# Joined hi/lo products of 512 and 256 columns in the up projections of four MLPs

## The chip, the cores and the metric

The kernel runs on one core of a Trainium2 chip. The metric is the device time in microseconds of one execution; three executions of the kernel before gave 1311.13, 1312.89 and 1314.19 us, median 1312.89.

## The reference

Two transformer stacks of two layers each work on one sequence of T = 256 tokens with D = 1024 features, in fp32. The first stack has a differential attention layer and a sparse attention layer (NSA), each modulated by a condition vector c; the second has a latent attention layer (MLA) and a block attention layer (MoBA). Each of the four layers ends in the same kind of MLP with 4096 hidden features, called m0 to m3 here:

```
h = rms_norm(x, g)                      # m0, m1: then h * (1 + scale) + shift
x = x + gate * (square(relu(h @ w1)) @ w2)   # m2, m3: no gate
```

scale, shift and gate come from `silu(c) @ ada_w + ada_b`, a vector times a matrix of 1024 x 6144 per layer of the first stack (and one of 1024 x 2048 for the shared keys and values).

## The kernel before

**Precision.** A float32 product is made from three fp32r products (L538 to L540, `product`): with a = a_hi + a_lo and b = b_hi + b_lo it sums a_hi b_hi, a_hi b_lo and a_lo b_hi in PSUM. Weights are split when they arrive. A piece is 128 partitions x 1024 floats (512 KB). SyncE loads it into a ring of ten slots (`wring`), ScalarE copies its rounded high part into a ring of five (`whi`, L2765, `split_high`), VectorE subtracts to get the low part (`wlo`, L1619, `split_low`), and that subtraction frees the slot of `wring`. A piece can be split once TensorE has read the piece five places earlier.

**An MLP.** The hidden features are worked in eight chunks of 512. `up(c)` makes the hidden values of chunk c (feature-major: 128 features on the partitions, 256 tokens on the columns), from four pieces of w1, each with two of the eight k tiles and four blocks of 128 features. It is `by_pairs` (L558): two PSUM banks of 512 columns, each with two feature blocks of 256 columns, 96 products of 256 columns in all. `down(c)` multiplies chunk c with four pieces of w2 into four accumulating outputs in `ps_s` and `ps_p`, 48 products of 512 columns. The order on TensorE is up(0), up(1), down(0), up(2), down(1), ..., up(7), down(6), down(7). So a chunk is eight pieces: four of w1, then four of w2.

Between up(c) and down(c), for each half of a chunk (256 features, one bank): ScalarE takes ReLU of the bank into `hidden` (a tile in `ex`, three halves deep, L2891), then squares it into `g_hi` (L2896); GpSimd squares the same values in place in fp32 (L3460); VectorE subtracts to get `g_lo` (L1873).

**VectorE's order.** `mlp` on VectorE is a loop over 64 positions j, one per piece. At position j it does what is due (the two `g_low` come at the two positions behind the last w1 piece of a chunk), then in m0 and for two chunks in m1 one modulation sum (`matvec`, L1630: a piece of ada_w times the silu row, accumulated), then it splits the piece four places ahead. In m0 the sums fill positions 0 to 47: twelve modulation chunks of four pieces. In m2 `bias_steps` (L2438) adds the position-bias lookup: at j % 8 == 2 the one-hot comparisons (L2443, L2445), at j % 8 == 5 the addition of the mask that drains the lookup's bank (L2453). On TensorE `lookup` (48 products of 32 columns, L752) is called between up(c) and down(c-1) for c of 2 and more.

**Loads.** SyncE issues the loads in a fixed order, each when its ring slot is free. In m0 groups of four weight pieces and four modulation pieces alternate, so that a chunk has 16 loads; a modulation piece's slot is freed by its sum on VectorE. In the other MLPs a chunk has eight loads (m1 also has two modulation groups).

**Banks.** The four banks of `bank` are taken in turn (`bank_take`): TensorE waits until the last use of the bank is drained. In an MLP before, each up chunk takes two and ScalarE's ReLU drains them.

## Time and profile before

| | |
|---|---|
| median of three executions | 1312.89 us |
| profiled execution, its own time | 1313.38 us |
| its span, first to last instruction | 1311.6 us |
| TensorE busy | 1258.9 us, 96% |
| VectorE busy | 860.6 us, 66% |
| ScalarE busy | 691.9 us, 53% |
| GpSimd busy | 136.9 us, 10% |
| mean granted clock of TensorE | 0.991 |

Matmuls overlap, so the busy time of TensorE isn't a measure of its peak; the distance from one start to the next is. In the profile PE is the matmul, PEld the weight load, DVE is VectorE, ACT ScalarE, POOL GpSimd and SPq the queue of SyncE. The MLPs lie at 167 to 353, 532 to 718, 826 to 1018 and 1129 to 1308 us of the span. A row of the timeline gives the start, the duration, the engine, the line and what was written from what; in brackets stands the idle time of the engine before it and what ended it.

### The profile page before, as it was taken

Reading aid. Unit: us, or ns where it says so; the run is one execution under the profiler, and the core shown is the slowest. Engines: PE = TensorE matmul, PEld = TensorE weight load, DVE = VectorE, ACT = ScalarE, POOL = GpSimd, SP = SyncE. Lnnn points to the kernel's source line nnn. Section 1 sums busy time; section 2 is a strip of 40 time slices with the busy share of each in tenths; the row PEclk is TensorE's granted clock in tenths of the full one; section 3 lists DMA queues with packets and bytes.
Section 4 is the critical chain, followed back from the end, with each engine's and each line's share of the span. In section 5 each row is a group of like instructions: output and inputs, shape, how many; then the busy total and the mean of one; then the engine's idle time right before and its main releaser. Section 6 shows DMA issues by size and latency. Waiting matters only on the chain.

```text
span 1311.6 us, 21556 instructions
## 1 busy us (share of the span) xinstructions
PE 1258.9 (96%) x8320; PEld 1092.7 (83%) x8320; DVE 860.6 (66%) x1501; ACT 691.9 (53%) x1219; POOL 136.9 (10%) x154
## 2 busy tenths in 40 slices
PE   6899999999999999999999989999999999999999
PEld 4798799889799656889898867889998778899997
DVE  6578699898675675786546774665565566654444
ACT  3466454445455665644445874644444565654542
POOL 1012121121100000100100320100100100010100
PEclk7899999999999999999999999999999999999999
DMA  9879569999489151585653522686554554466650
GB/s 365 327 261 324 182 217 372 359 339 371 156 243 293 49 177 65 181 315 185 190 170 109 177 94 79 153 324 181 174 179 142 176 177 138 153 183 200 180 160 32
DMA packets 123780, 267.37 MB, mean 204 GB/s; under 512 B 11040, under 2 KB 33824, under 8 KB 123296
## 3 DMA queue, kind: packets, MB, share of 16 engines
q1 hardware_dynamic: 119328, 257.23, 59.1%
q0 software_dynamic: 1728, 6.29, 1.5%
q10 hardware_dynamic: 2624, 2.49, 0.6%
q8 instruction: 66, 1.08, 0.3%
q14 instruction: 34, 0.28, 0.1%
HBM read 264.83 MB, written 1.15 MB: 203 GB/s over the span
## 4 chain that ended last, share of the span: by engine, by line
PE 63%; DVE 5%; ACT 3%; issue 1%; POOL 1%; DVEq 0%; ACTq 0%; POOLq 0%
PE bank L538 12%; PE bank L540 11%; PE bank L539 11%; PE ps_s L538 3%; PE ps_s L539 3%; PE ps_s L540 3%; PE ps_p L538 3%; PE ps_p L539 3%; PE ps_p L540 3%; PE ps_s L1324 1%; DVE wlo L1619 1%; PE ps_p L1167 1%; PE ps_p L1143 1%; POOL rs L3444 1%; PE ps_s L1131 1%
## 5 line engine op out<-in xcount | busy, mean ns | idle before, releaser
L1619 DVE TENSOR_TENSOR wlo<-wring,whi 128x1024 fp32r<-128x1024 f32 (+1 forms) x376 | 457.9, 1228 | 262.5 <-ACT whi L2765 258.3
L2765 ACT ACTIVATE whi<-wring 128x1024 fp32r<-128x1024 f32 (+1 forms) x376 | 388.2, 1045 | 359.2 <-PE bank L540 135.1
L538 PE MATMUL bank<-h_hi,whi 128*128 128x256 f32 (+1 forms) x1224 | 348.7, 285 | 4.9 <-DVE wlo L1619 1.8
L539 PE MATMUL bank<-h_lo,whi 128*128 128x256 f32 (+1 forms) x1224 | 346.2, 283 | 0.0
L540 PE MATMUL bank<-h_hi,wlo 128*128 128x256 f32 (+1 forms) x1224 | 346.2, 283 | 0.0
L538 PEld LDWEIGHTS bank<-h_hi,whi 128*128 128x128 f32 (+1 forms) x1224 | 233.9, 191 | 10.7 <-issue 8.9
L539 PEld LDWEIGHTS bank<-h_lo,whi 128*128 128x128 f32 (+1 forms) x1224 | 234.0, 191 | 0.8
L540 PEld LDWEIGHTS bank<-h_hi,wlo 128*128 128x128 f32 (+1 forms) x1224 | 234.0, 191 | 0.0
L3460 POOL TENSOR_TENSOR ex<-ex 128x512 f32<-128x512 f32 x64 | 81.6, 1278 | 666.5 <-ACT g_hi L2896 666.5
L538 PE MATMUL bank<-whi,h_hi 128*128 128x512 f32 (+2 forms) x232 | 93.5, 403 | 12.8 <-DVE wlo L1619 10.4
L538 PE MATMUL ps_s<-whi,g_hi 128*128 128x512 f32 x256 | 101.0, 394 | 0.6 <-DVE wlo L1619 0.6
L538 PE MATMUL ps_p<-whi,g_hi 128*128 128x512 f32 x256 | 100.1, 391 | 0.0
L539 PE MATMUL ps_s<-wlo,g_hi 128*128 128x512 f32 x256 | 99.9, 390 | 0.0
L540 PE MATMUL ps_s<-whi,g_lo 128*128 128x512 f32 x256 | 99.7, 390 | 0.0
L540 PE MATMUL ps_p<-whi,g_lo 128*128 128x512 f32 x256 | 99.7, 389 | 0.0
L539 PE MATMUL ps_p<-wlo,g_hi 128*128 128x512 f32 x256 | 99.6, 389 | 0.0
L1630 DVE CUSTOM_DVE_ANT_0 wring<-wring,wide,params 128x1024 f32<-128x1024 f32 x64 | 85.2, 1337 | 7.1 <-DMA wring<-in_ada_w_t 7.1
L540 PE MATMUL bank<-whi,h_lo 128*128 128x512 f32 (+2 forms) x232 | 88.9, 383 | 0.0
L539 PE MATMUL bank<-wlo,h_hi 128*128 128x512 f32 (+2 forms) x232 | 88.9, 383 | 0.0
L1873 DVE TENSOR_TENSOR g_lo<-ex,g_hi 128x512 fp32r<-128x512 f32 x64 | 46.3, 724 | 34.5 <-POOL ex L3460 34.5
L538 PEld LDWEIGHTS bank<-whi,h_hi 128*128 128x128 f32 x232 | 44.8, 193 | 24.1 <-issue 14.6
L538 PEld LDWEIGHTS ps_s<-whi,g_hi 128*128 128x128 f32 x256 | 48.1, 188 | 10.7 <-DVE wlo L1619 0.9
(391 smaller groups left out, 1763.5 us busy)
## 6 DMA issues: line engine op xcount, KB each, us to landing
wring<-in_mlp_w SPq DMA_DIRECT2D x128, 512.0 KB, 5.2
wring<-in_mlp_w_in SPq DMA_DIRECT2D x64, 512.0 KB, 3.9
wring<-in_mlp_w_out SPq DMA_DIRECT2D x64, 512.0 KB, 4.0
wring<-in_ada_w_t SPq DMA_DIRECT2D x48, 512.0 KB, 8.0
wring<-in_ada_w SPq DMA_DIRECT2D x36, 512.0 KB, 6.3
wring<-in_moba_w_qkv SPq DMA_DIRECT2D x24, 512.0 KB, 3.9
wring<-in_a_qk SPq DMA_DIRECT2D x16, 512.0 KB, 7.2
wring<-in_kv_ada_w_t SPq DMA_DIRECT2D x16, 512.0 KB, 6.9
```

The lines of the kernel that those rows point to most:

```text
L538: nc.tensor.matmul(out, lh, rh, start=first, stop=False, skip_group_check=mixed)
L539: nc.tensor.matmul(out, lh, rl, start=False, stop=False, skip_group_check=mixed)
L540: return nc.tensor.matmul(out, ll, rh, start=False, stop=last, skip_group_check=mixed)
L1131: last = nc.tensor.matmul(ps_s[:, m, lo:lo + n], q_t[rows, j, t * P:(t + 1) * P], k_nsa[rows, w, j // 2, 0:n], start=True, stop=True)
L1143: last = nc.tensor.transpose(ps_p[:, 0, i * P:(i + 1) * P], ex[:, 2 * (b % 2) + m, i * P:(i + 1) * P], ident[:, :])
L1167: last = nc.tensor.matmul(out_[m][:, lo:lo + n], v_nsa[:, w, i, g * 64:(g + 1) * 64], pt_nsa[b % 2][:, m, at:at + n], start=False, stop=(w ...
L1324: last = nc.tensor.matmul(ps_s[:, u % 2, lo:lo + n], q[:, t * P:(t + 1) * P], k[:, 0:n], start=(i == 0), stop=(i == len(parts) - 1))
L1619: v.tensor_tensor(piece_view(wlo, p), raw_view(p), piece_view(whi, p).bitcast(F32), ALU.subtract).then_inc(lo_ready, 1)
L1630: return v.tensor_tensor_reduce(w, w, c_row[:, :], 1.0, params[:, at:at + 1], ALU.mult, ALU.add, mod[:, 4 * i + j:4 * i + j + 1])
L1873: v.tensor_tensor(g_lo[at], hidden[:, b % 3, :].rearrange("p (i t) -> p i t", t=T), g_hi[at].bitcast(F32), ALU.subtract).then_inc(sem("mlp ...
L2765: a.activation(piece_view(whi, p), raw_view(p), ACT.Copy).then_inc(hi_ready, 1)
L3460: g_.tensor_tensor(h, h, h, ALU.mult).then_inc(sem("mlp_sq"), 1)
```

## The change

`h_hi` and `h_lo` become two halves of one tile, `h_both`. In all four MLPs `up(c)` is made by `by_halves`: each block of 128 features has a whole bank. The high weights are multiplied with high and low activations in one product of 512 columns (columns 0 to 255 get w_hi h_hi, columns 256 to 511 get w_hi h_lo), and the low weights with the high activations in one of 256 columns, added to the second half. A chunk has 64 products instead of 96, and takes all four banks.

The two halves of a bank must be added. ScalarE copies the second half into `rest` (in the tile `att`), VectorE adds the first half to it (`join`, at the position behind the last w1 piece), which drains the bank; ScalarE then takes ReLU in place and squares. `g_low` comes one position later. In m2 the lookup moves from ahead of down(c-1) into its middle, and the addition behind it from j % 8 == 5 to 3.

```diff
-        h_hi = sb("h_hi", [P, KT, T], F32R)
-        h_lo = sb("h_lo", [P, KT, T], F32R)
+        h_both = sb("h_both", [P, 2, KT, T], F32R)
+        h_hi, h_lo = h_both[:, 0, :, :], h_both[:, 1, :, :]
...
+        JOINED = ["m0", "m1", "m2", "m3"]
+        rest = att[:, 0:D].rearrange("p (i t) -> p i t", t=T)
...
+            def by_halves(key, ready=None):
+                banks = [bank_take(pe, key + (n,)) for n in range(4)]
+                for j in range(KT // 2):
+                    p = piece_wait()
+                    wh, wl = piece_view(whi, p), piece_view(wlo, p)
+                    for n in range(4):
+                        out = bank[:, banks[n], :]
+                        for k in (2 * j, 2 * j + 1):
+                            if ready and n == 0:
+                                ready(k)
+                            at = (slice(None), k % 2, slice(n * P, (n + 1) * P))
+                            nc.tensor.matmul(out, wh[at], h_both[:, :, k, :], start=(k == 0), stop=False,
+                                             skip_group_check=True)
+                            last = nc.tensor.matmul(out[:, T:2 * T], wl[at], h_hi[:, k, :], start=False,
+                                                    stop=(k == KT - 1), skip_group_check=True)
+                        if n < 3 and j == KT // 2 - 1:
+                            last.then_inc(filled[banks[n]], 1)
+                    piece_over(last, key + (3,) if j == KT // 2 - 1 else None)
...
-                def down(c):
+                def down(c, middle=None):
                     pe.wait_ge(sem("mlp_glo"), 16 * int(tag[1]) + 2 * c + 2)
                     if c < 7:
                         for k in range(4):
+                            if middle and k == 2:
+                                middle()
...
-                    if beside and c >= 2:
-                        beside(c - 2)
-                    down(c - 1)
+                    down(c - 1, (lambda: beside(c - 2)) if beside and c >= 2 else None)
...
+                def join(c):
+                    for n in range(4):
+                        i, key = 4 * c + n, (f"{tag}_w1", c, n)
+                        if n % 2 == 0 and 2 * c + n // 2 >= 3:
+                            dve.wait_ge(sem("mlp_glo"), 16 * int(tag[1]) + 2 * c + n // 2 - 2)
+                        dve.wait_ge(sem("mlp_rest"), 32 * JOINED.index(tag) + i + 1)
+                        src = bank_full(dve, key)
+                        v.tensor_tensor(hidden[:, (2 * c + n // 2) % 3, (n % 2) * T:(n % 2 + 1) * T], src[:, 0:T],
+                                        rest[:, i % 4, :], ALU.add).then_inc(drained[uses[key][0]], 1)
...
                 for j in range(64):
                     p = base + j
+                    if j in joins:
+                        join(joins[j])
                     if j in due:
                         g_low(due[j])
                     key = pieces[p][0]
                     if key[0].endswith("w1") and p == first_piece[key] + 3:
-                        due.update({j + 1: 2 * key[1], j + 2: 2 * key[1] + 1})
+                        behind = 2 if tag in JOINED else 1
+                        due.update({j + behind: 2 * key[1], j + behind + 1: 2 * key[1] + 1})
+                        if tag in JOINED:
+                            joins[j + 1] = key[1]
...
-                if j % 8 == 5 and 0 <= j // 8 - 2 < LOOKUPS:
+                if j % 8 == 3 and 0 <= j // 8 - 2 < LOOKUPS:
...
+            def joined_mlp(tag):
...
+                for c in range(8):
+                    for n in range(4):
+                        i, key = 4 * c + n, (f"{tag}_w1", c, n)
+                        src = bank_full(act, key)
+                        if c:
+                            bank_emptied(act, (f"{tag}_w1", c - 1, n))
+                        a.activation(rest[:, i % 4, :], src[:, T:2 * T], ACT.Copy).then_inc(sem("mlp_rest"), 1)
+                    for half in range(2):
+                        b = 2 * c + half
+                        for n in (2 * half, 2 * half + 1):
+                            bank_emptied(act, (f"{tag}_w1", c, n))
+                        h = hidden[:, b % 3, :]
+                        a.activation(h, h, ACT.Relu).then_inc(sem("mlp_relu"), 1)
+                        if c >= 2:
+                            act.wait_ge(*read_end[first_piece[(f"{tag}_w2", c - 2)] + 3])
+                        act.wait_ge(sem("mlp_relu"), 16 * JOINED.index(tag) + b + 1)
+                        a.activation(g_hi[:, c % 2, 2 * half:2 * half + 2, :], h.rearrange("p (i t) -> p i t", t=T),
+                                     ACT.Square).then_inc(sem("mlp_ghi"), 1)
```

## Rows read from the trace of the kernel before

**Rows 1.** The page: busy time and share by engine; the chain that ended last.
```profile
PE 1258.9 (96%) x8320; PEld 1092.7 (83%) x8320; DVE 860.6 (66%) x1501; ACT 691.9 (53%) x1219; POOL 136.9 (10%) x154
...
PE 63%; DVE 5%; ACT 3%; issue 1%; POOL 1%; DVEq 0%; ACTq 0%; POOLq 0%
```

**Rows 2.** Timeline of TensorE in m1: start and duration in us, line, what.
```profile
565.76 0.28 PE L538 MATMUL bank<-h_hi,whi 128*128 128x256 f32 x1
...
577.27 0.40 PE L538 MATMUL ps_s<-whi,g_hi 128*128 128x512 f32 x1
...
588.18 0.28 PE L538 MATMUL bank<-h_hi,whi 128*128 128x256 f32 x1
```

**Rows 3.** Windows of m0: length, busy time by engine, granted clock, DMA share, GB/s.
```profile
190.37:305.86 115.49, 113.08 (x722) 102.42 (x721) 107.05 (x128) 50.77 (x58) 17.83 (x10) 1.00 0.97 356
```

**Rows 4.** Waits from 165 to 370 us: in total, times, longest.
```profile
ACT whi L2765 <- DMA wring<-in_mlp_w: 71.2, 43, 6.2
...
DVE wlo L1619 <- ACT whi L2765: 19.0, 14, 3.1
```

**Rows 5.** 128x256 instructions from PSUM, VectorE and ScalarE: min/median/max ns.
```profile
L2498 DVE TENSOR_TENSOR h_lo<-ps_p,h_hi x8: 416/423/425, 778.6 to 815.1; 128x256 fp32r<-128x256 f32 x8
...
L3272 ACT ACTIVATE bias<-bank x8: 366/379/399, 746.9 to 771.9; 128x256 f32<-128x256 f32 x8
```

**Rows 6.** Timeline of VectorE in m0.
```profile
187.29 0.68 DVE L1873 TENSOR_TENSOR g_lo<-ex,g_hi 128x512 fp32r<-128x512 f32 x1
...
194.57 2.05 DVE L1619 TENSOR_TENSOR wlo<-wring,whi 128x1024 fp32r<-128x1024 f32 x1
...
264.39 2.06 DVE L1619 TENSOR_TENSOR wlo<-wring,whi 128x1024 fp32r<-128x1024 f32 x1
266.37 1.52 DVE L1873 TENSOR_TENSOR g_lo<-ex,g_hi 128x512 fp32r<-128x512 f32 x1
267.82 1.27 DVE L1630 CUSTOM_DVE_ANT_0 wring<-wring,wide,params 128x1024 f32<-128x1024 f32 x1
...
269.02 1.22 DVE L1619 TENSOR_TENSOR wlo<-wring,whi 128x1024 fp32r<-128x1024 f32 x1
270.16 0.68 DVE L1873 TENSOR_TENSOR g_lo<-ex,g_hi 128x512 fp32r<-128x512 f32 x1
...
280.65 1.23 DVE L1619 TENSOR_TENSOR wlo<-wring,whi 128x1024 fp32r<-128x1024 f32 x1 [1.58 <-ACT whi L2765]
...
312.10 2.05 DVE L1619 TENSOR_TENSOR wlo<-wring,whi 128x1024 fp32r<-128x1024 f32 x1
```

**Rows 7.** Timeline of ScalarE in m0, behind up(4).
```profile
262.07 0.58 ACT L2891 ACTIVATE ex<-bank 128x512 f32<-128x512 f32 x1
262.68 0.63 ACT L2896 ACTIVATE g_hi<-ex 128x512 fp32r<-128x512 f32 x1
263.22 0.58 ACT L2891 ACTIVATE ex<-bank 128x512 f32<-128x512 f32 x1
...
267.41 1.06 ACT L2765 ACTIVATE whi<-wring 128x1024 fp32r<-128x1024 f32 x1 [2.95 <-DMA wring<-in_mlp_w]
```

**Rows 8.** Timeline of GpSimd and VectorE in m1, behind up(0).
```profile
544.87 1.23 POOL L3460 TENSOR_TENSOR ex<-ex 128x512 f32<-128x512 f32 x1 [0.40 <-ACT g_hi L2896]
545.84 1.34 DVE L1619 TENSOR_TENSOR wlo<-wring,whi 128x1024 fp32r<-128x1024 f32 x1 [0.65 <-ACT whi L2765]
```

**Rows 9.** The page, loads of m2 and m3: count, KB each, us from issue to landing.
```profile
wring<-in_mlp_w_in SPq DMA_DIRECT2D x64, 512.0 KB, 3.9
```

**Rows 10.** Timeline of TensorE in m0, the first product of up(5).
```profile
270.38 0.36 PE L538 MATMUL bank<-h_hi,whi 128*128 128x256 f32 x1 [0.84 <-DVE wlo L1619]
```

**Rows 11.** Timeline of VectorE in m2, chunk 2: one-hot pair, next split, bias addition.
```profile
881.20 0.81 DVE L2443 TENSOR_SCALAR extra<-arena,cmp_w 128x2048 f16<-128x2048 f16 x1
...
883.30 1.23 DVE L1619 TENSOR_TENSOR wlo<-wring,whi 128x1024 fp32r<-128x1024 f32 x1
...
889.51 0.68 DVE L2453 TENSOR_TENSOR bias<-bank,wide 128x512 f32<-128x512 f32 x1
```

More of the change, by code:

```diff
@@ L576, in by_pairs @@
                     piece_of[key + (g,)] = p
+            def by_halves(key, ready=None):
[17 more added lines that the diff above has]
+                for n in range(4):
+                    piece_of[key + (n,)] = p
             def by_token(key, src, kt, readers=1, first_k=0, between=None, apart=False, step=None):
@@ L761, in up @@
                 def up(c):
+                    if tag in JOINED:
+                        by_halves((f"{tag}_w1", c), (lambda k: wait(tag, k)) if c == 0 else None)
+                        return
                     by_pairs((f"{tag}_w1", c), (h_hi, h_lo), (lambda k: wait(tag, k)) if c == 0 else None)
@@ L1865, in mlp @@
                 base = first_piece[(f"{tag}_w1", 0)]
-                due = {}
+                due, joins = {}, {}
+                def join(c):
[7 more added lines that the diff above has]
+                                        rest[:, i % 4, :], ALU.add).then_inc(drained[uses[key][0]], 1)
                 def g_low(b):
@@ L2882, in attention @@
                             copy(u - 1)
+            def joined_mlp(tag):
+                if tag in x_sums:
+                    act.wait_ge(sem("x_squared"), 2 * list(x_sums).index(tag) + 2)
+                for c in range(8):
+                    for n in range(4):
+                        i, key = 4 * c + n, (f"{tag}_w1", c, n)
[14 more added lines that the diff above has]
+                                     ACT.Square).then_inc(sem("mlp_ghi"), 1)
+                keep_ahead("act", first_piece[(f"{tag}_w2", 7)])
             def mlp(tag):
+                if tag in JOINED:
+                    joined_mlp(tag)
+                    return
                 for b in range(2 * FF // W):
```

1 line of the change is left out of this document (added).

## The prediction

> **What bounds the kernel now.** I read the busy times first, then the chain, then TensorE's order of time inside one MLP, and last the waits and timelines of VectorE and ScalarE in the first MLP. TensorE is busy for 96% of the span, and 63% of the chain that ended last is its own [rows 1]. In the second MLP it runs without a gap: 96 products of an up chunk from 565.76 to 577.27, 48 of a down chunk from there to 588.18 [rows 2]. The third and fourth MLPs repeat this. The first MLP differs: five chunks take 115.49 us, where 11.51 + 10.91 each [rows 2] would make 112.1, with the DMA engines 97% busy [rows 3], ScalarE waits 71.2 us there for weights, and VectorE 19.0 us for ScalarE's high parts [rows 4]. TensorE, the DMA stream and VectorE are all close to their limit in it. So the change has to be priced per MLP.
>
> **TensorE: three products become two.** Before, 96 products of 256 columns take 11.51 us, 119.9 ns each; 48 of 512 columns take 10.91 us, 227.3 ns each [rows 2]. At the full granted clock of 2.4 GHz [rows 3] the columns alone would be 106.7 and 213.3 ns. Each product thus costs some 13.2 to 14.0 ns on top of its columns, whatever its width. The new pair (512, then 256) streams the same 768 columns in 227.3 + 119.9 = 347.2 ns against 359.7: 12.5 ns less, in 8 chunks x 32 pairs x 4 MLPs = 1024 pairs, 12.8 us in all, 3.2 us an MLP, 0.4 us a chunk. Nothing in the trace shows a 512-column operand read as two runs of 256 far apart. Bounds: all 12.8 us, or nothing if that reading costs the 12.5 ns again. I take the full gain, because the two widths agree on the fixed part.
>
> **ScalarE and VectorE: the added work.** Per chunk ScalarE gets four 128x256 copies (379 ns each), VectorE four 128x256 additions from PSUM (416 to 425 ns) [rows 5]. VectorE's consecutive instructions start some 0.08 us before the end of the previous one (a 680 ns g_lo costs 0.60 [rows 6]), so four joins occupy 1.36 us. ScalarE has room everywhere (53% busy [rows 1]). The second new thing is order. ReLU now waits for a join, and the high part of the piece behind the chunk is queued on ScalarE behind two ReLUs and two squares. By the steps of before (0.61 and 0.54 us from start to start [rows 7]; an SBUF source makes the first about 0.63) ScalarE starts that high part 2.4 us after it is released by the second join, it takes 1.06 us [rows 7], and 0.1 us later VectorE can subtract. I cost this at nothing in the second and fourth MLP: TensorE has four split pieces in hand when the join begins (one down chunk, 10.9 us [rows 2]), VectorE is through after about 5 us. g_lo of the last chunk comes about 8 us after the last up product and is needed after 10.9. The copies run while the last piece of the chunk is still multiplied. These two MLPs gain 3.2 us each.
>
> **The first MLP.** Here each of 48 positions of VectorE's loop also holds a modulation sum. One position, subtraction and sum, is 2.34 us (267.82 to 270.16: 1.20 and 1.14) [rows 6]. A chunk of eight is 18.7, with two g_lo of 0.60 each 19.9. GpSimd's squares slow two VectorE instructions a chunk: 2.06 instead of 1.22, 1.52 instead of 0.68, 1.7 us in all. The rest, 1.58 and more at the first piece of a w2 group, is a wait for weights [rows 6]. From 194.57 to 312.10 five chunks take 117.5, 23.5 each [rows 6].
> After: 19.9 + 1.36 of joins. Then VectorE runs joins 3 and 4 and one sum (1.9 us) against ScalarE's chain of 3.7 us, and idles 1.8. But GpSimd's squares now fall mostly into that idle time. In the second MLP, where a subtraction starts at 545.84 while GpSimd works from 544.87 to 546.10, it takes 1.34 instead of 1.22 [rows 8]; I take 0.2 us a chunk instead of 1.7. That makes 23.3. The wait for weights: a load issued when its ring slot is freed lands after 3.9 us if little is queued [rows 9], its high part adds 1.3, and VectorE has 4.7 us of other work before it needs it: 0.5 us at least. The queue adds to it. A chunk is 16 loads of 0.524 MB, at 356 GB/s and 97% share [rows 3] 22.9 us of full use; VectorE's longer first half lets the queue drain, and I get 0.1 to 0.3 more. So 24.0 us a chunk against 23.5, though 3 us were added. Bounds of the chunk: 23.5, if the transfers alone pace it; 26.4, if the 1.7 of GpSimd stays and the wait for weights is 1.6 as before.
> At the start, g_lo of the second half moves behind one more position and the join: it comes at 191.9 instead of 187.97 [rows 6], TensorE starts its first down product at 192.0 instead of 190.37, and VectorE is 0.8 us late four positions on. TensorE then follows VectorE: it has lost its margin, as it waited 0.84 us for a subtraction before already [rows 10]. From there 4.6 chunks x 0.5 = 2.3 more, and the last up chunk, behind the sums, gives 0.4 back: 0.8 + 2.3 - 0.4 = **+2.7 us**. By the bounds: +0.4 and +13.7.
>
> **The third MLP.** The bucket lookup (48 products, 1.2 us) moves from behind the up chunk to the middle of the down chunk, since all four banks are taken until the joins are through, and VectorE's bias addition from the sixth to the fourth position of a chunk. The next up chunk now asks for all four banks at once, the lookup's among them. With TensorE's end of the up chunk as zero, VectorE goes: joins to 1.0, subtraction from 4.1 (ScalarE's chain), g_lo, subtraction, g_lo, subtraction to 8.8, the one-hot pair 2.10 (881.20 to 883.30 [rows 11]) to 10.9, subtraction to 12.1, bias addition 0.68 [rows 11] to 12.8. TensorE wants the banks at 10.91 + 1.2 + 0.1 = 12.2. That is 0.7 us of stall in five chunks (the sixth lookup is followed by no up chunk), 3.5 us, bounds 0 and 1.2 each. The MLP changes by -3.2 + 3.5 = **+0.3 us** (-3.2 to +2.8).
>
> **Sum.** +2.7 - 3.2 + 0.3 - 3.2 = -3.4 us on the profiled execution's 1313.38 (span 1311.6 and 1.8 around it). The median of before is 0.5 lower; the same step from it gives **1309.5 us**.
>
> **A rule of the Trainium skill on the first step.** The rows give some 13 ns of fixed cost per product [rows 2]. The Trainium skill, TensorE: Matmul & The Clock Gate, section "Wait — 56ns, not 53.3ns?", puts the fixed part of a warm product at about 2.5 ns. By that page the joined pair would save 2.5 ns, 2.6 us over the kernel instead of 12.8, 0.65 an MLP, and the kernel would come out near 1317.5. The measured rows decide for my sum; the trace doesn't show whether the 13 ns belong to the product or to the weight load ahead of it, but both go from three to two.
>
> **The rivals.**
> *VectorE becomes the bound of the first MLP by more (slower).* GpSimd's squares keep slowing VectorE by 1.5 us a chunk more than I take: a cycle of 25.5. Then 0.8 + 4.6 x 2.0 - 0.4 = +9.6 there, in sum +3.5: 1316.5 us. For it: VectorE is already busy 107.1 of 115.5 us [rows 3]. Against: its new idle time lies where GpSimd works. It decides above 24.7 us a chunk.
> *The joined product gains nothing (slower).* The two far runs cost the 12.5 ns again, or the fixed cost isn't one of the product. Then +3.1 + 0 + 3.5 + 0 = +6.6: 1319.5 us. For it: no row shows such an operand. Against: the fixed part is the same at both widths.
> *The transfers pace the first MLP and the lookup's bank is in time (faster).* +0.4 - 3.2 - 3.2 - 3.2 = -9.2: 1303.7 us. For it: the DMA engines are 97% busy [rows 3], so VectorE's waits could swallow all the joins; the bias addition misses by 0.7 us only. Against: the waits seen (19.0 us [rows 4]) lie in the other half of the chunk than the new ones.
>
> **How the numbers follow.** Forecast 0.5, with a range of its own from 1306 to 1314; VectorE bound 0.25; no gain on TensorE 0.08; all hidden 0.17. Range with 8 in 10: 1304 to 1318. A measurement of this kernel tells about 0.2%, 2.6 us, from no change. Of the forecast's half, 0.29 lies below that and 0.19 inside; the hidden case is faster; the two slower ones leave 0.04 inside. Faster 0.46, within 0.23, slower 0.31.
>
> **What would show it.** Up chunks of the second and fourth MLP 11.1 us instead of 11.5, with no gap. The first down product of the first MLP near 192, and VectorE's cycle there near 24.0, with idle time behind the joins. In the third MLP a wait of TensorE for VectorE's bias addition, of some 0.7 us, five times. It would be wrong if the up chunks stay at 11.5, if the second or fourth MLP shows waits for split weights or g_lo, or if the cycle of the first is 25 or more.

## The result, and the profile after

The changed kernel takes 1329.8 us (median of 1328.6, 1331.6, 1331.0 and 1325.9), the kernel before 1313.5 beside it: a ratio of 1.0111, 95% interval 1.0093 to 1.0129. I had forecast 1309.5 with a range of 1304 to 1318. It is slower by 16 us, outside the range and on the wrong side.

The page after: busy time by engine, and the chain of work that ended last.
```profile
PE 1256.6 (95%) x7296; PEld 1038.3 (78%) x7296; DVE 883.9 (67%) x1629; ACT 731.7 (55%) x1347; POOL 122.6 (9%) x154
...
PE 58%; DVE 8%; ACT 3%; issue 2%; POOL 1%; DVEq 0%; ACTq 0%; POOLq 0%
```
Compared with [rows 1], TensorE issues 1024 products fewer and yet is busy almost as long; VectorE's share of the chain rises from 5 to 8%. Where the time went is read best from the first product of each MLP in the two timelines:

| | before starts | after starts | this MLP and what lies behind it | forecast |
|---|---|---|---|---|
| m0 | 167.26 | 167.36 | +10.8 | +2.7 |
| m1 | 531.74 | 542.64 | 0.0 | -3.2 |
| m2 | 826.35 | 837.26 | +4.5 | +0.3 |
| m3 | 1128.77 | 1144.17 | -0.2 | -3.2 |

Three readings lie under it. First, TensorE in m0 behind up(0), and VectorE in the same stretch (start, duration, what; in brackets the idle time before it and what ended it):
```profile
178.50 0.28 PE L594 MATMUL bank<-h_both,wlo 128*128 128x256 f32 x1
...
182.83 1.41 DVE L1903 TENSOR_TENSOR ex<-bank,att 128x256 f32<-128x256 f32 x4
...
184.50 0.76 PE L592 MATMUL bank<-h_both,whi 128*128 128x512 f32 x1 [5.72 <-DVE ex L1903]
...
185.27 0.63 PE L592 MATMUL bank<-h_both,whi 128*128 128x512 f32 x1
185.70 0.41 PE L594 MATMUL bank<-h_both,wlo 128*128 128x256 f32 x1
185.91 0.63 PE L592 MATMUL bank<-h_both,whi 128*128 128x512 f32 x1
```
up(1) follows up(0) directly, and its first product waits for all four banks, hence for all four joins of chunk 0. VectorE reaches them only at 182.83, behind its sums and splits. The same wait is there in the other MLPs, 1.2 to 1.3 us each. I had no such term at all: the first two up chunks take 31.04, 24.20, 24.00 and 24.00 us, against 23.11 before. The wait costs more than its 5.7 us: behind it the pairs come 0.64 us apart (185.27 to 185.91) and not 0.35. The granted clock says why. The window from 167.30 to 190 (length, busy PE, PEld, DVE, ACT, POOL, granted clock, DMA share, GB/s) has it at 0.85:
```profile
167.30:190.00 22.70, 16.92 (x81) 14.54 (x82) 20.81 (x33) 11.66 (x17) 2.29 (x2) 0.85 0.67 229
```

Second, TensorE in m1, one up chunk (as [rows 2]):
```profile
599.98 0.39 PE L592 MATMUL bank<-h_both,whi 128*128 128x512 f32 x1
...
611.27 0.40 PE L540 MATMUL ps_s<-whi,g_hi 128*128 128x512 f32 x1
```
11.29 us for 32 pairs, 352.8 ns each, where I had 347.2. The pair saves 6.9 ns and not 12.5.

Third, ScalarE and VectorE in m0 around a chunk's end:
```profile
268.31 1.19 ACT L2937 ACTIVATE att<-bank 128x256 f32<-128x256 f32 x4
...
271.81 1.41 DVE L1903 TENSOR_TENSOR ex<-bank,att 128x256 f32<-128x256 f32 x4
...
272.65 0.63 ACT L2943 ACTIVATE ex<-ex 128x512 f32<-128x512 f32 x1 [3.16 <-DVE ex L1903]
...
275.16 2.94 ACT L2808 ACTIVATE whi<-wring 128x1024 fp32r<-128x1024 f32 x3
...
276.31 1.23 DVE L1646 TENSOR_TENSOR wlo<-wring,whi 128x1024 fp32r<-128x1024 f32 x1 [1.89 <-ACT whi L2808]
```
ScalarE stands 3.16 us for VectorE's joins, and after the two Relus and Squares VectorE stands 1.89 us for ScalarE's high half. The waits of 165 to 370 us say how much that is in all:
```profile
ACT whi L2808 <- DMA wring<-in_mlp_w: 46.7, 25, 7.2
DVE wlo L1646 <- ACT whi L2808: 31.9, 22, 4.2
...
ACT ex L2943 <- DVE ex L1903: 18.7, 6, 4.5
```
ScalarE waits less for loads than in [rows 4] (46.7 for 71.2), VectorE more for ScalarE (31.9 for 19.0), and the wait of 18.7 is new.

### The profile page after: what moved, and what is told of

Same layout as the page of the kernel before. It is cut to its first block, busy times and chain, and to the rows that moved or that the text cites. A ratio compares the mean times of both kernels' runs of the same rounds, so it can differ in the third digit from the quotient of the medians.

```text
span 1326.8 us, 20048 instructions
## 1 busy us (share of the span) xinstructions
PE 1256.6 (95%) x7296; PEld 1038.3 (78%) x7296; DVE 883.9 (67%) x1629; ACT 731.7 (55%) x1347; POOL 122.6 (9%) x154
## 4 chain that ended last, share of the span: by engine, by line
PE 58%; DVE 8%; ACT 3%; issue 2%; POOL 1%; DVEq 0%; ACTq 0%; POOLq 0%
PE bank L592 14%; PE bank L594 7%; PE bank L540 5%; PE bank L542 4%; PE bank L541 4%; PE ps_s L540 3%; PE ps_s L542 3%; PE ps_s L541 3%; PE ps_p L542 3%; PE ps_p L540 3%; PE ps_p L541 3%; DVE wlo L1646 2%; PE ps_s L1351 1%; ACT whi L2808 1%; PE ps_p L1194 1%
## 5 line engine op out<-in xcount | busy, mean ns | idle before, releaser
L592 PE MATMUL bank<-h_both,whi 128*128 128x512 f32 x1024 | 365.9, 401 | 21.7 <-DVE ex L1903 9.6
L594 PE MATMUL bank<-h_both,wlo 128*128 128x256 f32 x1024 | 288.3, 282 | 0.0
L592 PEld LDWEIGHTS bank<-h_both,whi 128*128 128x128 f32 x1024 | 193.5, 189 | 73.9 <-issue 26.8
L594 PEld LDWEIGHTS bank<-h_both,wlo 128*128 128x128 f32 x1024 | 194.6, 190 | 0.6
L3530 POOL TENSOR_TENSOR ex<-ex 128x512 f32<-128x512 f32 x64 | 67.9, 1063 | 700.8 <-ACT g_hi L2947 700.0
L540 PE MATMUL bank<-whi,h_both 128*128 128x512 f32 (+2 forms) x232 | 93.6, 403 | 13.2 <-DVE wlo L1646 10.7
L541 PE MATMUL bank<-wlo,h_both 128*128 128x512 f32 (+2 forms) x232 | 89.0, 384 | 0.0
L542 PE MATMUL bank<-whi,h_both 128*128 128x512 f32 (+2 forms) x232 | 89.0, 384 | 0.0
L540 PEld LDWEIGHTS bank<-whi,h_both 128*128 128x128 f32 x232 | 44.9, 193 | 24.3 <-issue 14.8
L540 PE MATMUL bank<-h_both,whi 128*128 128x256 f32 (+1 forms) x200 | 58.6, 293 | 0.0
L2937 ACT ACTIVATE att<-bank 128x256 f32<-128x256 f32 x128 | 46.9, 380 | 17.7 <-PE bank L594 17.2
L541 PE MATMUL bank<-h_both,whi 128*128 128x256 f32 (+1 forms) x200 | 56.5, 282 | 0.0
```

The lines of the kernel that those rows point to most:

```text
L540: nc.tensor.matmul(out, lh, rh, start=first, stop=False, skip_group_check=mixed)
L541: nc.tensor.matmul(out, lh, rl, start=False, stop=False, skip_group_check=mixed)
L542: return nc.tensor.matmul(out, ll, rh, start=False, stop=last, skip_group_check=mixed)
L592: nc.tensor.matmul(out, wh[at], h_both[:, :, k, :], start=(k == 0), stop=False, skip_group_check=True)
L594: last = nc.tensor.matmul(out[:, T:2 * T], wl[at], h_hi[:, k, :], start=False, stop=(k == KT - 1), skip_group_check=True)
L2937: a.activation(rest[:, i % 4, :], src[:, T:2 * T], ACT.Copy).then_inc(sem("mlp_rest"), 1)
```

## The experiments

The table gives for each kernel the ratio to the kernel before (95% interval), and from its profile m0: its first two up chunks, the rest to the end of the last up product, and their sum, in us. All the stretches are read from the starts of TensorE's products. The ratio rests on all executions of a kernel, the stretches on the profiled one alone.

| kernel | ratio | first two | rest | sum |
|---|---|---|---|---|
| before | 1 | 23.1 | 138.2 | 161.3 |
| changed | 1.0111 (1.0093-1.0129) | 31.0 | 140.2 | 171.3 |
| e1 banks one by one | 1.0068 (1.0049-1.0088) | 28.7 | 146.3 | 175.0 |
| e2 chunk 0 plain | 1.0034 (1.0017-1.0052) | 23.6 | 144.5 | 168.1 |
| e3 m0 old | 1.0034 (1.0023-1.0046) | 23.1 | 138.0 | 161.1 |
| e4 sums later | 1.0127 (1.0110-1.0144) | 24.0 | 140.3 | 164.3 |
| e5 splits first | 1.0044 (1.0028-1.0059) | 30.0 | 138.1 | 168.2 |
| e6 m0 old, banks one by one | 0.9981 (0.9971-0.9991) | 23.6 | 136.9 | 160.5 |
| e7 contiguous | 0.9983 (0.9968-0.9998) | 23.1 | 136.8 | 159.9 |
| e9 plain and splits | 1.0024 (1.0011-1.0038) | 22.9 | 146.7 | 169.6 |
| e10 one split | 1.0042 (1.0027-1.0057) | 22.9 | 149.1 | 172.0 |
| e11 wide first | 0.9939 (0.9922-0.9956) | 23.1 | 138.1 | 161.2 |
| e13 joined, short sums | 0.9949 (0.9932-0.9967) | 23.5 | 133.4 | 156.8 |
| e14 old, short sums | 0.9954 (0.9938-0.9969) | 23.6 | 134.5 | 158.1 |
| e15 joined, short loads | 1.0008 (0.9996-1.0021) | 30.0 | 135.7 | 165.8 |
| e16 old, short loads | 0.9951 (0.9935-0.9967) | 23.1 | 134.5 | 157.6 |

Two rows can therefore differ by some microseconds without their kernels doing so. e1's six executions lie between 1318.9 and 1326.6 us, with mean granted clocks of 0.991 and 0.986 at the two ends, and the profiled one is the slowest; e2's twelve lie between 1313.4 and 1323.7, and the profiled one took 1315.2. A part of this is TensorE's clock. In e1 two up chunks of m0, in e2 and e4 one, have a mean granted clock of 0.87 and take 12.74 to 12.77 us, where the others at 1.00 take 11.29 to 11.65. In e2 the wait ahead of the slow one is
```profile
224.82 0.50 PE L594 MATMUL bank<-h_both,whi 128*128 128x512 f32 x1 [1.87 <-DVE wlo L1648]
```
The same is seen between m1 and m2. That stage runs wholly at the full clock in the profiles of before, of the changed kernel, of e2 and of e3; in the other twelve a part near 760 to 800 us is at the lower level, and the stage is 1.6 or 3.2 us longer. Whether a change brings that about isn't shown.

**e1, banks one by one.**
```diff
-                banks = [bank_take(pe, key + (n,)) for n in range(4)]
+                banks = []
...
+                        if j == 0:
+                            banks.append(bank_take(pe, key + (n,)))
```


> The changed kernel, but each of the four banks of an up chunk is taken (and waited for) just before its own first product, not all four before the first product of the chunk. Theory: the up chunk that directly follows another up chunk (chunk 1 behind chunk 0, once an MLP) waits for the fourth and last join of chunk 0, 1.2 to 1.3 us in m1, m2 and m3 and 5.7 us in m0. A join needs 0.35 us, and the second bank is wanted only 0.7 us (two pairs) after the first: so the wait falls by the three later joins, 1.05 us in m0 (4.7 us stay, since VectorE only gets to the first join that late) and by all of 1.2 us in each of the other three. Total -4.7 us, 1325.1 us, a ratio to before of 1.0075 instead of 1.0111. Rival: VectorE and ScalarE pace the chunks and the wait at the start only moves lateness that comes back at the first down product; then less than 1 us comes back in all, 1329 us, ratio 1.0107.


Measured: 1323.8 us. TensorE's waits from 540 to 1010 us (m1, m2 and what lies between) held two rows for banks in the changed kernel:
```profile
PE bank L592 <- DVE bias L2496: 4.0, 5, 0.9
PE bank L592 <- DVE ex L1903: 2.5, 2, 1.3
```
In e1 the first row is gone and the second is down to 0.2 us. m1 (to its last up product) and m3 gave 1.2 and 1.3 us, as expected, though the stage behind m1 took 3.1 us more in this profile, by the clock; m2 gave 5.9, because the lookup's bank is now wanted last of four and its bias addition is in time. m0 did the opposite: 2.4 us gained on the first two chunks, 6.1 lost behind them. Of the 6.1, the two up chunks at 0.87 are 3.0, and TensorE's waits for low halves, 8.2 us for 5.6, are most of the rest. The bank wait is shown as the cause for m1 to m3, and for m0 not beyond its start. The 1325.1 us of the forecast came out near, but by other parts: more in m2, less in m0.

**e2, chunk 0 in the old way** (two banks, three products, Relu from the bank), on top of e1.
```diff
-                    if tag in JOINED:
+                    if tag in JOINED and c:
                         by_halves((f"{tag}_w1", c))
...
-                for c in range(8):
+                for b in range(2):
...
+                    a.activation(hidden[:, b, :], src, ACT.Relu).then_inc(drained[uses[key][0]], 1)
...
+                    a.activation(g_hi[:, 0, 2 * b:2 * b + 2, :], hidden[:, b, :].rearrange("p (i t) -> p i t", t=T),
+                                 ACT.Square).then_inc(sem("mlp_ghi"), 1)
+                for c in range(1, 8):
```


> The kernel of the experiment before, and chunk 0 of each MLP is made in the old way (three products of 256 columns a pair, two banks, Relu straight from the bank by ScalarE, no rest copies and no joins); chunks 1 to 7 stay joined. Theory: the changed kernel's first two up chunks cost 31.0 us in m0 and 24.0 in the others, against 11.5 + 11.3 = 22.8 without a wait for banks. m1, m2 and m3 give 1.2 us each. In m0 TensorE's stall of 5.7 us goes, but VectorE is next: between its joins of chunk 0 (182.83) and chunk 1 (198.13) it needed 15.3 us for four positions, where a chunk of eight takes 24.7; without the stall four positions are 12.3 us, and the four joins of chunk 0 (1.4 us) go, so join 1 comes 4.4 us earlier and all of m0 with it. Total -8.0 us: 1321.8 us, ratio 1.0050. Rival 1, VectorE's own load is all of m0's loss: only the 1.4 us of its joins go there, 1324.8 us. Rival 2, the bank wait was the whole loss of m0: the first down product comes at 191.0 instead of 198.4 and stays 7.4 us ahead, 1318.8 us.


Measured: 1318.3 us. The start of m0 is repaired (23.6), but 144.5 us follow where the changed kernel had 140.2. Of 7.5 us gained, 3.2 stay. One up chunk at the lower clock is 1.5 of the 4.3 lost, 2.0 are longer waits for low halves (7.5 us for 5.6). So the forecast of 4.4 us for m0 was too high; 1321.8 us was beaten because it left out the 4 us behind m2's lookups.

**e3, m0 as before.** `JOINED = ["m1", "m2", "m3"]`


> The changed kernel with m0 left as it was before (m1, m2 and m3 joined). Theory: m0 starts at the same time in both traces and ends 10.9 us later in the changed one, so all of that comes back and nothing else moves: 1318.9 us, ratio 1.0028, and what stays (+3.5 to +5 us) is m2. Rival: the lateness of m0 is partly made up by transfers that run ahead meanwhile, which the later stages then lack when it is gone; then 3 to 5 us of the 10.9 stay, 1322 to 1324 us.


Measured: 1317.7 us, ratio 1.0034 for the 1.0028 expected; m1 starts at 531.47. All of m0's loss comes back, and nothing is lost elsewhere for it.

**e4, sums later.**
```diff
-    plan += mix(mlp("m0"), ada(0, range(10, 12)) + ...)
+    m0 = mlp("m0")
+    plan += m0[:2] + mix(m0[2:], ada(0, range(10, 12)) + ...)
...
-            mlp("m0", ada_order[10:22], last=...)
+            mlp("m0", ada_order[10:22], last=..., first=8)
```


> The changed kernel, but the twelve sums of m0 begin behind chunk 1 (VectorE's positions 8 to 55 instead of 0 to 47, their loads behind the second up chunk), as m1's two do. Theory: TensorE's 5.7 us wait in m0 is there because VectorE does four sums (1.28 us each) and four splits (1.23 us) ahead of the first join; without the sums it is at that join when the bank is full, and the wait is the 1.2 us of m1. The eight first positions then take 24.0 us in place of 31.0; but eight sums move into a chunk that had none (22.3 us then, 24.7 with sums), so 2.4 us come back later: -4.6 us, 1325.2 us, ratio 1.0076. Rival: TensorE waits for the joins as such, not for the sums ahead of them: the wait stays near 5.7 us, and only the order of the sums changes, 1330 to 1332 us.


Measured: 1331.0 us. The reading of the trace was right and the forecast wrong: the wait fell to 1.2 us (24.0 for the first two chunks), so it was the sums ahead of the join. But 8 us came back behind the last up chunk, where sums now lie: m1 starts at 543.49, in the changed kernel at 542.64. Part of that is clock again: the window from 345 to 375 us has it at 0.83, the changed kernel from 353 to 383 at 0.94. The rival's 1330 to 1332 us was met, but not for its reason, since the wait did fall. Here the repaired start was worth nothing by itself.

**e5, one high half ahead of each Relu**, on top of e1.
```diff
                     for half in range(2):
                         b = 2 * c + half
+                        keep_ahead("act", first_piece[(f"{tag}_w1", c)] + 4 + half)
```


> The kernel with banks taken one by one (m0 joined, first sums at position 0), and ScalarE copies one high half of a later piece ahead of the first Relu of a chunk and one ahead of the second, instead of all of them behind both pairs of Relu and Square. Theory of a handshake: in m0 of the changed kernel ScalarE is through with the rest copies of a chunk at 269.5, stands 3.16 us in front of Relu until VectorE's four joins (271.81), then does 2.7 us of Relu and Square, and only then the next high half (275.16), for which VectorE in turn stands 1.89 us (276.31): once a chunk, each waits for the other. Over m0 VectorE's idle time in front of its low halves grew from 19.0 to 31.9 us, while its busy time did not grow: that 12.9 us is the 10.9 us of m0. With a high half ready ahead of Relu the wait of 1.9 us goes in seven chunks: 8 to 11 us of m0 come back, 1314 to 1316 us, ratio about 1.001. Rival 1, transfers: in the same stretch the DMA engines are busy 0.93 of the time, and the slots in which loads land come free as VectorE works; then the wait only turns into one for a load, and less than 3 us come back, 1321 to 1324 us. Rival 2, VectorE's added joins (32 x 0.35 = 11.3 us) are the loss: nothing comes back.


Measured: 1320.2 us. VectorE's waits of 165 to 365 us:
```profile
DVE g_lo L1913 <- POOL ex L3533: 11.1, 11, 1.1
DVE wlo L1648 <- ACT whi L2810: 10.8, 14, 2.6
```
Its wait for high halves fell from 34.8 us in e1 to 10.8, and the stretch behind the first two chunks from 146.3 to 138.1. From m0's start to m1's it is 371.2 us for 378.6. But the ratio, over all executions, fell by 0.0024 only, 3.2 us: e1's profile is of its slowest execution. The forecast of 8 to 11 us missed, and 3.2 is close to the first rival's less than 3. A new wait of 11.1 us for GpSimd's square came in.

**e9 and e10, both repairs, and one split only.** e9 is e2 with e5's line; e10 has `+ 4` for `+ 4 + half`.


> Both repairs of m0 together: chunk 0 in the old way (no wait of up chunk 1 for joins) and one high half ahead of each of the two Relus of a chunk; banks one by one, all four MLPs joined. Theory (two separate losses that add up): the profile with the splits moved had 138.1 us for m0's chunks behind the first two, as before's 138.2, but 30.0 us for the first two, where the one with a plain chunk 0 had 23.6 and before 23.1. Together 23.6 + 138.1: m0 takes what it took before, and m1, m2, m3 are 1.2, 1.1 and 1.3 us shorter than before. Sum -3 us against before: 1310 to 1311 us, ratio 0.9977; against the kernel with m0 left old it is a tie. Rival: m0's chunks are held up by VectorE's total work whatever the order, and once the start is early the lateness comes back behind it, as with banks one by one (2.4 us gained at the start, 6.1 us lost behind it); then 138 becomes 142 to 145 us, and the ratio is 1.002 to 1.004.

> As the one before, but only one high half of a later piece ahead of the first Relu of a chunk, none ahead of the second. In the profile with both, VectorE stood 11.1 us (11 times, up to 1.1) in front of the difference of a half block for GpSimd's square, which it never did in the changed kernel: the second copy makes the second Square 1.06 us late. Theory: with one copy only, that wait goes, and VectorE's wait for high halves (10.8 us with both, 31.9 with none) grows less than that, since the next piece is already there: m0 is 1 to 3 us shorter than in the experiment beside it, ratio 0.996. Rival: the waits change places one for one, the two kernels agree within 1 us.


Measured: 1318.9 and 1322.1 us. The repairs don't add: with the start at 22.9 us, the rest took 146.7 and 149.1, the rival's case in e9. In e10 the wait for GpSimd fell from 9.2 to 7.3 us and that for high halves rose from 15.7 to 19.6; both forecasts for e10 missed. By then seven kernels with joined m0 had ended it at 164 to 175 us, the one of 164 giving it back later, and what sets that total was still open.

**e13 to e16, less work for VectorE or fewer bytes, in joined and in old m0.** In e13 and e14 m0's modulation sums take 128 of 1024 columns; in e15 and e16 their loads bring 128 of them, and the sums stay whole. Part of the modulation is left out in all four.
```diff
-                ins = mod_block(key, j, loaded(load)[:, 0, :])
+                ins = mod_block(key, j, loaded(load)[:, 0, 0:P] if key in ada_order[10:22] else ...)
...
+                if key in ada_order[10:22]:
+                    to, src = to[:, :, 0:P], src[:, :, 0:P]
                 sp.dma_start(to, src)
```


> All four MLPs joined, banks one by one; VectorE's sums of m0 take only 128 of their 1024 columns (part of the modulation is left out), their loads stay whole. So VectorE has about 1.1 us less to do in each of 48 positions. Theory VectorE: what holds joined m0 is that VectorE comes late to the joins and splits; then the start wait goes (22.9 us for the first two chunks) and the rest is set by the loads as before's m0 was: 160 to 162 us from m0's start to its last up product where the kernel with whole sums has 171 to 175; -11 to -14 us of 1323.8, 1310 to 1313 us, ratio 0.998. Theory transfers: the slots come free later only because loads come later; m0 stays at 168 us or more, ratio 1.004 or more.

> m0 old, m1 to m3 joined, banks one by one, and the same short sums. Theory: before's m0 is set by its loads (DMA engines busy 0.97 of the time) and not by VectorE: from its start to the last up product 160 to 161 us as with whole sums (161.3), ratio 0.998 as with whole sums. Rival: VectorE's work (166 us busy of the 171 to 198) is what sets it already before; then it falls to the 157.6 us of m1's pace, -4 us, ratio 0.995.

> All joined, banks one by one, and the sums' loads bring only 128 of their 1024 columns (the sums run over all columns of what lies in the slot; part of the modulation is left out), so m0's transfers fall from 58.7 to some 36 MB. Theory VectorE: VectorE does as much as before and waits no less in front of the first joins, but the loads come in time: the waits for high halves that come from late loads go, and VectorE's busy time of 164 us with the start wait remains; 165 to 170 us to the last up product, ratio 1.003. Theory transfers: m0 falls to TensorE's pace, 22.9 + 133.4 = 156 to 158 us, ratio 0.995.

> m0 old with the same short loads, m1 to m3 joined. Theory: the loads set before's m0, so it falls to TensorE's pace of 23.1 + 134.5 = 157.6 us from 161.3, if VectorE (153 us of busy time in these 48 positions and behind them) lets it: ratio 0.995. Rival: VectorE set it; it stays at 161 us, ratio 0.998.


Windows of 190 to 310 us (length, busy PE, PEld, DVE, ACT, POOL, granted clock, DMA share, GB/s), for the changed kernel,
```profile
190.00:310.00 120.00, 116.08 (x583) 97.10 (x583) 103.74 (x148) 58.12 (x79) 11.34 (x10) 1.00 0.91 328
```
e13, joined with short sums,
```profile
190.00:310.00 120.00, 120.00 (x601) 101.34 (x600) 76.67 (x158) 67.32 (x89) 12.48 (x12) 1.00 1.00 380
```
and e15, joined with short loads:
```profile
190.00:310.00 120.00, 119.90 (x606) 101.02 (x605) 108.33 (x152) 60.12 (x81) 11.36 (x10) 1.00 0.60 199
```
With short sums and every byte still loaded, joined m0 takes 156.8 us, TensorE has no gap, and the DMA engines bring 380 GB/s. So the transfers could do more than either kernel asked of them, and the DMA share of 0.91 is not their limit. Joined and old m0 are then about even (156.8 and 158.1 us, where old m0 loses 0.5 at its start at a clock of 0.98; 1307.3 and 1308.0 us for the whole kernels).

With short loads and whole sums the start still costs 30.0 us, 4.0 of it the wait for the joins. VectorE's sums ahead of the first joins are its cause, as e4 says too. Behind the start it is different: 135.7 us, where e1 had 146.3, the changed kernel 140.2, and e13 133.4. There fewer bytes help nearly as much as fewer sums, though VectorE does all its work. So neither VectorE's work nor the bytes alone hold up these chunks, but both together. That fits the ring, though no run separates its parts: a slot comes free when VectorE is through with it, and through ScalarE VectorE waits for what lands in it. From e1, whose edit both kernels have, the ratio falls by 0.0119 with short sums and by 0.0060 with short loads.

Joined m0 with short loads (165.8) stays 8.1 us behind old m0 (157.6). Old m0 misses TensorE's pace of 157.6 us by 2.3 to 3.7 with whole sums and whole loads, and by 0.5 or none when either is cut. My forecast for e14, that only the loads set it, was wrong, and so was the same idea in e13, where I had 160 to 162 us for joined m0.

**e6, m0 old with e1's edit; e7, the two halves of h side by side; e8 and e12, products alone; e11, another order.** e6 joins `["m1", "m2", "m3"]`; e7 has `h_both = sb("h_both", [P, KT, 2, T], F32R)` on top of e6.


> m0 in the old way, m1, m2 and m3 joined with their banks taken one by one. From the profiles of the two experiments this is put together of: m0 as before; m1 and m3 1.2 and 1.5 us shorter than before (22.9 and 133.4 us against 23.1 and 134.5), m2 1.1 us shorter, since taking the banks one by one also took away the 0.8 us that TensorE stood behind each of five lookups (the lookup's bank is the last of the four that the next up chunk takes). Theory: these add up, -3.8 us, 1310 us, ratio 0.9971. Rival: what the first up chunks give comes back later, as m0's did, and the kernel is as before, ratio 1.000.

> The kernel of the experiment before with the high and the low half of a k tile of h side by side in memory (one run of 512 columns) instead of 8 KB apart (two runs of 256). Theory: the 5.6 ns that a joined pair costs above the 347.2 ns of my sum are the jump between the two runs; then up chunks fall from 11.29 to 11.11 us (64 pairs instead of 64 times 352.8 ns: 22.2 to 22.58), 24 chunks, -8.6 us at 352.8 - 347.2 = 5.6 ns for 32 x 2 pairs a chunk, that is 0.36 us each where TensorE paces them; 1301 to 1306 us. Rival: a product's cost above its columns does not depend on where its columns lie; pairs stay at 352.8 ns and the time equals that of the experiment before within 1 us.

> Only products, nothing of the reference is computed: TensorE alone, stretches of 64 pairs each (three products of 256 columns; 512 + 256 with the 512 in two runs; 512 + 256 with them side by side; 512 and 256 into two banks; 512 alone in two runs, 512 alone side by side, 256 alone, 384 alone; then the first two kinds again). Theory from the two traces: three products cost 359.7 ns and the joined pair 352.8 ns here too, without any other engine at work; if each product costs its columns and the same 13.2 ns, 512 alone is 226.5, 384 alone 173.2 and 256 alone 119.9 ns and the joined pair would be 346.4; so either 512 alone comes out at 232.9, or the pair costs more than its two parts. Rival 1: the 6 ns are the jump between two runs, 512 side by side is 226.5 and in two runs 232.9. Rival 2: they are the second product's partial write into the bank just written: into two banks the pair is 346.4. Rival 3: they come from the other engines' traffic, and the pair alone is 346.4.


e6 took 1311.5 us, 0.9981 for the 0.9971 expected. In its profile m1 (to its last up product), m2 and m3 are 1.2, 1.0 and 1.3 us shorter than before, so the parts add up; the stage behind m1 is 3.2 us longer, by the clock. e7 took 1311.8, no difference, and its up chunks stay at 11.29. (Its forecast counted 64 pairs a chunk; there are 32, so the theory was worth 4.3 us and not 8.6. It fails either way.) e8's timeline at the borders of its stretches (64 pairs or products each, all at a granted clock of 1.00; `far` is the operand in two runs, `near` in one):
```profile
63.40 0.40 PE L78 MATMUL bank<-far,w_hi 128*128 128x512 f32 x1
...
86.01 0.40 PE L83 MATMUL bank<-near,w_hi 128*128 128x512 f32 x1
...
108.63 0.40 PE L88 MATMUL bank<-far,w_hi 128*128 128x512 f32 x1
...
131.24 0.40 PE L93 MATMUL bank<-far,w_hi 128*128 128x512 f32 x1
...
145.77 0.39 PE L97 MATMUL bank<-near,w_hi 128*128 128x512 f32 x1
...
160.28 0.28 PE L101 MATMUL bank<-far,w_hi 128*128 128x256 f32 x1
...
167.95 0.34 PE L105 MATMUL bank<-near,w_hi 128*128 128x384 f32 x1
...
179.05 0.28 PE L72 MATMUL bank<-far,w_hi 128*128 128x256 f32 x1
...
202.08 0.40 PE L78 MATMUL bank<-far,w_hi 128*128 128x512 f32 x1
```
Divided by 64: the pair 353.3 ns in two runs, 353.4 in one, 353.3 into two banks; 512 alone 227.0 in two runs and 226.7 in one, 256 alone 119.8, 384 alone 173.4, three of 256 together 359.8. The parts are what I took. The pair in turn costs 6.5 ns more than its parts, with no other engine at work; all three rivals fall.


> Only products again, nothing of the reference; 128 in a stretch, each into its own columns of a bank with its own weights: 512 and 256 in turn, by twos, by fours, by eights, then 512 and 384, 512 and 128, 256 and 128 in turn, 128 alone, and three of 512 to one of 256. Theory: a change of length costs 3.3 ns a change, whichever way: 512 and 256 in turn 353.3 ns for two, by twos 350.0, by fours 348.4, by eights 347.6; three to one 227.0 x 3 + 119.8 + 6.5 = 807.3 ns for four. Rival 1: it is the load of weights that must fit beside the product ahead of it: then 256 behind 512 is cheap and 512 behind 256 dear, and the sums are the same, but 512 and 384 in turn cost no extra (400.4 ns for two). Rival 2: products in turn always cost 3.3 ns each, in any grouping: by eights 353 ns.


e12, in ns for one of each: 512 and 256 in turn 353.4, by twos 348.4, by fours 350.9, by eights 349.1 (parts 346.8); 512 and 384 in turn 413.1 (parts 400.4); 512 and 128 in turn 339.4, 256 and 128 in turn 231.4, 128 alone 111.6 (parts 338.6 and 231.4); three of 512 to one of 256, 812.8 for four (parts 800.8). Grouping is cheaper than turn about, but there is no price per change of length: twos beat fours, and 512 with 384 costs 12.7 ns extra where 512 with 256 costs 6.5. That refutes the theory (348.4 ns by fours, 347.6 by eights) and both rivals (no extra with 384; 353 ns by eights). What it is stays open.
In e11 the 512s of a piece go ahead of its 256s (the code is shortened):
```diff
+                    turns = [(0, 1), (2, 3)] if j == KT // 2 - 1 else [(0, 1, 2, 3)]
+                    for ns in turns:
+                        for n in ns:
+                            for k in ks:
+                                nc.tensor.matmul(bank[:, banks[n], :], wh[at], h_both[:, :, k, :], ...)
+                        for n in ns:
+                            for k in ks:
+                                last = nc.tensor.matmul(bank[:, banks[n], T:2 * T], wl[at], h_hi[:, k, :], ...)
```


> m0 old, m1 to m3 joined with banks one by one, and the products of a piece in another order: the eight of 512 columns first, then the eight of 256 (in the last piece of a chunk four and four, so that the first banks are full early). Theory from products alone: 512 columns again and again cost 227.0 ns, 256 again and again 119.8, but the pair in turn 353.3 ns, 6.5 ns more than its parts; so it is the change of length from one product to the next that costs, and eight and eight pay it once, not eight times: 5.5 ns less a pair, 32 pairs in 8 chunks of three MLPs, 4.2 us less than the same kernel with pairs in turn: up chunks of 11.11 us for 11.29, 1307.3 us, ratio 0.9950. Rival: the extra is there for any product of 256 columns that adds into a bank's second half between others, in any order; then the chunks stay at 11.29 us and the ratio at 0.998.


In e11's m1 an up chunk is
```profile
564.62 0.39 PE L596 MATMUL bank<-h_both,whi 128*128 128x512 f32 x1
...
575.78 0.40 PE L540 MATMUL ps_s<-whi,g_hi 128*128 128x512 f32 x1
```
11.16 us, 4.1 ns less a pair. I had expected 5.5; e12's groups of eight say 4.3. 1308.1 us, ratio 0.9939 (0.9922 to 0.9956): the lowest ratio of all, and the fastest of the kernels that leave nothing out. Its profile is 3.1 us shorter than e6's; the ratios say 5.5, but their intervals together allow 3.1.

## Why the prediction was wrong

From the start of m0 to the end the profile is 15.1 us longer where I had 3.4 shorter. Of that difference 8.1 us lie in m0, 3.2 in m1, 4.2 in m2 and 3.0 in m3.

**The step that failed: "I cost this at nothing".** In the part on the added work of ScalarE and VectorE I followed the join into the down chunk, where TensorE has four split pieces in hand, and never into the chunk pair up(0), up(1), where no down chunk lies between. There TensorE wants the banks at once. It cost 1.2 to 1.3 us in each of m1 to m3, which e1 took away, and in m0 5.7 us of waiting and some 2.6 more at the lower clock behind it. I had seen the banks asked for all at once in m2 and priced it only there.

**The first MLP, +2.7 for +10.8.** Of the 10.8 us, 7.9 lie in the first two up chunks (31.04 for 23.11) and 2.9 behind them. I took the first down product at 192.0, 1.6 us later than before, and it came at 198.40. The 7.9 are the wait for the joins and what came of it. e13, with a wait of 0.7 there, takes 23.5, so 22.8 without any. 31.0 less 22.8 and less 5.7 leaves some 2.6 us. That fits the stretch up to 190 us in which the pairs came 0.64 us apart for 0.35.

The walk of VectorE itself was near in its parts: the second g_lo at 192.36 for 191.9, joins of 1.41 us, an idle time of 1.8 to 1.9 us in front of the next high half behind six of the eight joins, GpSimd's squares no longer in the way (the two g_lo of a chunk take 0.68 to 0.69 us; [rows 6] has one of 1.52). From join to join its cycle was 24.2 to 25.3 us, 24.6 on average, for the 24.0 I had. That is just short of the 24.7 from which I let the rival of a bound VectorE begin. The rival's +9.6 for m0 lies close to the +10.8 by luck: nearly all of it is a cycle 2.0 us longer in each chunk. The cycle was 1.1 us longer (24.6 for 23.5), and of TensorE's 10.8 us only 2.9 lie behind the start.

What sets joined m0 is shown for the start: VectorE's sums ahead of the first joins (e4 and e13 take the wait to 1.2 and 0.7 us, e15 leaves 4.0). Behind the start it is VectorE's sums and the loads together, each of which gives most of it back when cut (e13, e15). Another order alone did not mend it: e1, e2, e4, e5, e9 and e10 all stay above the kernel before. Why the chunks behind an early start take longer (144.5 to 149.1 in e2, e9 and e10, for 138.1 and 140.2 in e5 and the changed kernel) is settled in part. TensorE stands 7.5, 8.3 and 11.0 us there for low halves, against 2.4 and 5.6, and one, two and one of its up chunks run partly at the lower clock (one in e5 too). Why VectorE is late with the low halves isn't settled; from 190 to 310 us the DMA share is 0.89 to 0.92 in all five.

**The pair: right mechanism, wrong size.** 12.5 ns expected, 6.9 measured, 1.8 us an MLP for 3.2. I added the costs of two products measured each among its own kind; in turn they cost 6.5 ns more. The rival of no gain is wrong as well, and the reason it gave, two far runs, is refuted by e7 and e8. The Trainium skill's rule from the prediction (TensorE: Matmul & The Clock Gate, section "Wait — 56ns, not 53.3ns?": some 2.5 ns of fixed cost) isn't what these products show, each with its own weight load: 13.1 ns above the columns at 256, 13.7 at 512. Of the pair's saving it would have left 2.5 ns, and 6.9 were measured.

**The third MLP, +0.3 for +4.5.** The stall behind the lookup was there, five times, 0.8 us for 0.7 (my own terms, 12.8 less 12.2, give 0.6). VectorE and TensorE at that place:
```profile
920.13 0.68 DVE L2496 TENSOR_TENSOR bias<-bank,wide 128x512 f32<-128x512 f32 x1
...
921.07 0.47 PE L592 MATMUL bank<-h_both,whi 128*128 128x512 f32 x1 [0.67 <-DVE bias L2496]
```
The rest is the pair's size (1.4 us), the wait behind up(0) (1.2) and the lookups themselves: in the middle of a down chunk each takes 1.35 us (e1, m2 against m1), and 1.22 before.

**Second and fourth MLP, -3.2 for 0.0 and -0.2.** The pairs cost 1.4 us more than I had, the one bank wait 1.2 to 1.3, and the down chunks take 10.94 to 10.95 us for 10.91.

## What to carry to other kernels

Where a change takes more buffers at once, look for the place where two producers follow each other with nothing between, and take each buffer just before its own first use; here that was worth 1.2 to 1.3 us in three of the MLPs and 4 us behind the lookups. A stage in which an engine is busy 93% of the time, and hands work to another in a fixed order, is no place for work moved off TensorE: price it by how often each waits for the other, and by what a wait of TensorE costs in clock, and leave it out if in doubt. When two resources are both close to their limit, cut each by itself before naming one as the cause. Before two profiles are compared, see where each lies among the executions of its kernel. Measure an operation in the sequence in which it will run, not among its own kind.

## What the hardware showed that I had not expected

Products of 512 columns cost 227 ns among themselves and products of 256 cost 120, but in turn 353.3 for the two, and 512 with 384 in turn 12.7 ns more than their parts. With weights of its own a product of 128 columns costs 111.6 ns, hardly less than one of 256. Reading the operand as two runs 8 KB apart costs at most 0.3 ns. After the wait of 5.7 us in m0 the granted clock is 0.85 in the window 167.3 to 190 and 1.00 in the next one, against 1.00 in both before: below 1.00 means that a part of that stretch ran at the lower of the two levels, 1.2 GHz. Behind waits of 1.9 us (e2) and 1.8 and 1.9 us (e1) for a low half it fell as well, and the up chunk then took 1.5 us more. So a wait of TensorE can cost 1.5 to 2.6 us on top of its own length. Not every wait was followed by the lower level: in the changed kernel's m0 three of 1.5 to 1.9 us were not.
